# mLSTM heads: exponential from PSUM, row spread by one float32r product, last head in two parts, diagonal masked by a minimum on VectorE

## The reference, cut to what matters

```python
lf = jax.nn.log_sigmoid(f_pre)                       # bb: its running sum
log_d = bb[..., :, None] - bb[..., None, :] + ib[..., None, :]
log_d = jnp.where(tri, log_d, -jnp.inf)
m_t = jnp.maximum(log_inter, jnp.max(log_d, axis=-1))
w_intra = jnp.exp(log_d - m_t[..., None])
s = jnp.einsum('bhtd,bhsd->bhts', qb, kb) * w_intra
num = ... + jnp.einsum('bhts,bhse->bhte', s, vb)
den = ... + jnp.sum(s, axis=-1)
h = num / jnp.maximum(jnp.abs(den), jnp.exp(-m_t))[..., None]
hh = rmsnorm(hh.transpose(0, 2, 1, 3), head_g)
return (hh * jax.nn.sigmoid(og)) @ w_out
```

## Time and profile before

| | us |
|---|---|
| median of 3 runs | 2892.79 (2875.12 to 2896.78) |
| profiled execution | 2877.44 |
| its span | 2875.7 |
| TensorE busy | 2755.7 (96%) |
| VectorE busy | 1515.8 (53%) |
| ScalarE busy | 866.6 (30%) |
| GpSimd busy | 357.9 (12%) |
| the heads' stage, from its first instruction to the next stage | 87.7 |

### The profile page before, as it was taken

One profiled execution on the slowest core, in us unless ns is written; L12 is line 12 of the kernel. 1 busy time (PEld: TensorE's weight loads), 2 busy tenths in 40 slices (PEclk: granted clock), 3 DMA queues, 4 the chain that ended last, 5 costly groups with the idle time before them and its releaser, 6 DMA issues. The chain is left out here.

```text
span 2875.7 us, 38965 instructions
## 1 busy us (share of the span) xinstructions
PE 2755.7 (96%) x16683; PEld 2189.1 (76%) x16683; DVE 1515.8 (53%) x2117; ACT 866.6 (30%) x1156; POOL 357.9 (12%) x334
## 2 busy tenths in 40 slices
PE   7999999899899999999999998999999899999998
PEld 5888878588675787788887875788887665788887
DVE  4555454689757634555545325452454655452433
ACT  3222233422343222322123435322222434422221
POOL 1111010211100000111100002120121100120110
PEclk9999999899999999999999997999999999999999
DMA  5554542000211123455553210233342200233231
GB/s 154 156 175 153 170 138 62 25 4 4 83 45 44 37 88 96 131 164 169 161 164 119 88 60 3 71 103 110 110 148 94 81 31 1 73 103 103 88 103 59
DMA packets 264316, 271.14 MB, mean 94 GB/s; under 512 B 9631, under 2 KB 245126, under 8 KB 263951
## 3 DMA queue, kind: packets, MB, share of 16 engines
q1 hardware_dynamic: 248784, 206.78, 23.6%
q0 software_dynamic: 15360, 61.87, 6.4%
HBM read 266.53 MB, written 2.10 MB: 93 GB/s over the span
## 5 line engine op out<-in xcount | busy, mean ns | idle before, releaser
L920 DVE TENSOR_TENSOR mix_wl<-ring_raw,mix_wh 128x2048 fp32r<-128x2048 f32 (+2 forms) x66 | 153.1, 2319 | 221.6 <-ACT mix_wh L807 221.5
L707 PE MATMUL mix_ps<-h_mix_hi,mix_wh 128*128 128x512 f32 x624 | 244.9, 392 | 0.0
L709 PE MATMUL mix_ps<-h_mix_lo,mix_wh 128*128 128x512 f32 x624 | 243.0, 389 | 0.0
L807 ACT ACTIVATE mix_wh<-ring_raw 128x2048 fp32r<-128x2048 f32 (+2 forms) x66 | 117.6, 1782 | 212.5 <-PE mix_ps L713 162.1
L707 PE MATMUL ffn_ps<-h_rw_hi,ffn_wh 128*128 128x512 f32 x448 | 175.4, 392 | 0.0
L709 PE MATMUL ffn_ps<-h_rw_lo,ffn_wh 128*128 128x512 f32 x448 | 174.3, 389 | 0.0
L920 DVE TENSOR_TENSOR mlp_wl<-ring_raw,mlp_wh 128x2048 fp32r<-128x2048 f32 (+1 forms) x38 | 96.7, 2545 | 130.3 <-ACT mlp_wh L807 130.3
L920 DVE TENSOR_TENSOR mlp_wl<-mlp_raw,mlp_wh 128x2048 fp32r<-128x2048 f32 x36 | 93.2, 2589 | 133.2 <-ACT mlp_wh L807 133.2
L713 PE MATMUL mix_ps<-h_mix_hi,mix_wl 128*128 128x512 f32 x624 | 154.2, 389 | 0.0
L707 PE MATMUL mlp_ps<-view,mlp_wh 128*128 128x512 f32 x384 | 149.8, 390 | 0.0
L709 PE MATMUL mlp_ps<-view,mlp_wh 128*128 128x512 f32 x384 | 149.5, 389 | 0.0
(11 more groups left out here) (605 smaller groups left out, 6107.5 us busy)
## 6 DMA issues: line engine op xcount, KB each, us to landing
ring_raw<-in_mlp_w SPq DMA_DIRECT2D x32, 1024.0 KB, 5.3
mlp_raw<-in_mlp_w SPq DMA_DIRECT2D x32, 1024.0 KB, 5.2
ffn_sraw<-in_ada_w POOLq DMA_DIRECT2D x34, 768.0 KB, 5.2
ffn_raw<-in_ffn_w_gu SPq DMA_DIRECT2D x44, 512.0 KB, 5.2
ring_raw<-in_ffn_w_gu SPq DMA_DIRECT2D x44, 512.0 KB, 4.8
mix_sraw<-in_ada_w POOLq DMA_DIRECT2D x22, 768.0 KB, 5.2
ring_raw<-in_w_in SPq DMA_DIRECT2D x14, 1024.0 KB, 5.3
ring_raw<-in_a_w_in SPq DMA_DIRECT2D x12, 1024.0 KB, 5.3
```

The lines of the kernel that those rows point to most:

```text
L707: nc.tensor.matmul(ps[:, it.banks[t], :], w(h, k, t), xh[:, k, :], start=it.first and k == it.k0, stop=False)
L709: nc.tensor.matmul(ps[:, it.banks[t], :], w(h, k, t), xl[:, k, :], start=False, stop=False)
L807: nc.scalar.activation(slot(wh, it), slot(raw, it), ACT.Copy).then_inc(hi_ready, 1)
L920: nc.vector.tensor_tensor(slot(wl, it), slot(raw, it), slot(wh, it).bitcast(F32), ALU.subtract)\
```

## The change

- The row -M is split in the gates' stage into a high part (float32r) in partitions 0 to 7 and the remainder in partitions 32 to 39, over a cleared tile. One float32r product with a selector of 40 rows (`sel2`) spreads both and adds them. The selector, the triangle and the floors as columns (`fcol`) are prepared in the gates' stage instead of at the start of the heads.
- ScalarE takes the exponential directly from the spread row in PSUM, with the column c[s] as its bias. The argument on VectorE and the copy `negM` are gone; `dT` has six buffers.
- The diagonal block of `dT`, not of `pT`, is cut by a minimum with the 0/1 triangle, on VectorE, two units ahead. GpSimd has nothing to do in the stage. The largest valid exponential is 1.
- Columns, and the reciprocal, are computed once per group, in groups of heads 0-2, 3-4, 5-6 and 7. Seven tables give the places of broadcasts, turns, copies, squares, roots, columns, scales and gates.
- The last head is done in two halves; its second half is read from PSUM. The sqrt table is loaded by an activation on one column after the last exponential. 3 keep-clock products stand at the start instead of 4 and 6, and 4 before the last turns.

```diff
@@ mlstm_gates
+            if at == first + 5:
+                sp.wait_ge(act_done, 6)
+                sp.dma_start(sel_in, I["c_sel2"]).then_inc(sel_loaded, 16)
+                sp.dma_start(causal, I["c_causal"]).then_inc(sel_loaded, 16)
...
+            if at == first + 5:
+                eng.wait_ge(floors, 2)
+                for t in range(TT):
+                    last = nc.tensor.transpose(pf[:, t, :], floor_rows[:, t * P:(t + 1) * P], e.ident[0:H, 0:H])
+                last.then_inc(turned, 1)
...
+            if at == first + 5:
+                eng.wait_ge(turned, 2)
+                nc.scalar.activation(fcol[:, :, :].rearrange("p h t -> p t h"), pf[:, :, :], ACT.Copy)
+            if at == first + 8:
+                eng.wait_ge(sel_loaded, 32)
+                nc.scalar.activation(sel, sel_in, ACT.Copy)
...
-                nc.vector.tensor_scalar(rows[:, 0, :], M[:, :], -1.0, None, ALU.mult).then_inc(dve_done, 1)
+                then(eng, nc.vector.memset(parts.bitcast(F32), 0.0))
+                nc.vector.tensor_scalar(neg[:, :], M[:, :], -1.0, None, ALU.mult).then_inc(dve_done, 1)
+            if at == first + 4:
+                eng.wait_ge(dve_done, 2)
+                then(eng, nc.vector.tensor_copy(parts[0:H, :], neg[:, :]))
+                nc.vector.tensor_tensor(parts[32:32 + H, :], neg[:, :], parts[0:H, :].bitcast(F32), ALU.subtract)
@@ tables
-MH_GROUPS = ((0, 1, 2), (3, 4), (5, 6, 7))
-MH_ROOTS = {(4, 0): 0, (6, 0): 1}
-MH_TURNS = {(4, 2): 0, (5, 0): 1, (5, 2): 2, (6, 2): 3, (7, 0): 4}
+MH_GROUPS = ((0, 1, 2), (3, 4), (5, 6), (7,))
+MH_BROADCASTS = {(0, 0): (1,), (0, 3): (2,), (2, 0): (3,), (3, 1): (4,), (4, 2): (5,), (5, 2): (6,), (6, 0): (7,)}
+MH_TURNS = {(4, 3): (0,), (5, 2): (1,), (6, 3): (2,), (7, 0): (3, 4), (7, 2): (5,)}
+MH_TAKES = {(2, 1): 0, (3, 0): 1, (3, 2): 2, (4, 3): 3, (5, 1): 4, (6, 3): 5, (7, 1): 6}
+MH_SQUARES = {(2, 2): 0, (3, 2): 1, (3, 3): 2, (5, 1): 3, (5, 3): 4, (7, 0): 5, (7, 2): 6}
+MH_ROOTS = {(4, 3): 0, (6, 3): 1}
+MH_COLUMNS = {(3, 2): 0, (5, 3): 1, (7, 1): 2}
+MH_SCALES = {(4, 2): (0,), (5, 1): (1, 2), (6, 2): (3, 4), (7, 2): (5, 6)}
+MH_GATES = {(5, 0): 0, (6, 2): 1, (6, 3): 2, (7, 0): 3, (7, 1): 4}
@@ mlstm_heads, tensor
                 if h > 0:
-                    pe.wait_ge(rows_out, h)
-                nc.tensor.matmul(pm[:, :], sel[:, h, :], rows[:, 0, :], start=True, stop=True).then_inc(rows_done, 1)
+                    pe.wait_ge(d_ready, TT * h)
+                nc.tensor.matmul(pm[:, :], sel[:, h * P:(h + 1) * P], parts, start=True, stop=True).then_inc(rows_done, 1)
...
-            for t in range(TT):
-                last = nc.tensor.transpose(pt[:, t * H:(t + 1) * H], rows[:, 1, t * P:(t + 1) * P], e.ident[0:H, 0:H])
-            last.then_inc(floors, 1)
-            keep_clock(nc, e, pn[:, 1, 1, :], 4)
-            pe.wait_ge(loaded, 32)
             broadcast(0)
             scores(0)
             scores(1)
-            keep_clock(nc, e, pn[:, 1, 1, :], 6)
+            keep_clock(nc, e, pn[:, 1, 1, :], 3)
...
-                pe.wait_ge(p_masked, n + 1)
+                pe.wait_ge(p_ready, n + 1)
...
-            for k in left:
-                turn(k)
+            pe.wait_ge(scaled, end)
+            turn(end - 1)
+            keep_clock(nc, e, pS[:, 1, :], 4)
+            for half in range(2):
+                pe.wait_ge(scaled, end + half + 1)
+                turn(end, (2 * half, 2 * half + 1))
@@ mlstm_heads, scalar
+                act.wait_ge(rows_done, h + 1)
+                if n >= ARGS:
+                    act.wait_ge(p_ready, n - ARGS + 1)
+                nc.scalar.activation(dT[:, n % ARGS, j * P:L], pm[:, j * P:L], ACT.Exp, bias=ccol[:, j, h:h + 1])\
+                    .then_inc(d_ready, 1)
+                if n + 1 == len(units):
+                    nc.scalar.activation(warm[:, :], e.eps[:, 0:1], ACT.Sqrt)
...
+            root(2)
+            act.wait_ge(used, TT * end + 2)
+            nc.scalar.activation(outT[:, end, 0:2, :], blocks_of(end)[:, 0, :, :], ACT.Copy).then_inc(taken, 1)
+            for i in range(2):
+                square(end, i, blocks_of(end)[:, 0, i, 0:P])
+            act.wait_ge(last_taken, 1)
+            for i in range(2):
+                square(end, 2 + i, blocks_of(end)[:, 1, i, 0:P])
+            root(3)
@@ mlstm_heads, vector
-                nc.vector.tensor_scalar(dT[:, n % 3, j * P:L], negM[:, h % 2, j * P:L], ccol[:, j, h:h + 1], 0.0,
-                                        ALU.add, ALU.min).then_inc(arg_ready, 1)
+            def mask(n):
+                dve.wait_ge(d_ready, n + 1)
+                j = units[n][1]
+                diag = dT[:, n % ARGS, j * P:(j + 1) * P]
+                nc.vector.tensor_tensor(diag, diag, causal, ALU.min).then_inc(d_masked, 1)
...
+            gate(end - 2)
+            dve.wait_ge(used, TT * H)
+            nc.vector.tensor_copy(outT[:, end, 2:4, P], blocks_of(end)[:, 1, :, P]).then_inc(last_taken, 1)
+            dve.wait_ge(last_taken, 1)
+            columns(3)
+            gate(end - 1)
+            scale(end, slice(0, 2))
+            scale(end, slice(2, TT), blocks_of(end)[:, 1, :, 0:P])
+            gate(end)
@@ mlstm_heads, gpsimd: the block is gone
-                nc.gpsimd.tensor_tensor(diag, diag, causal[:, :], ALU.mult).then_inc(p_masked, 1)
```

More of the change, by code:

```diff
@@ L1229, in shape_tables @@
     t["c_sel"] = sel.reshape(A_HEADS, -1)
+    sel2 = np.zeros((ROW_PARTS, A_HEADS * P), f32)
+    for part in range(2):
+        sel2[32 * part:32 * part + A_HEADS] = t["c_sel"]
+    t["c_sel2"] = sel2
     inv = (10000.0 ** (-np.arange(32, dtype=f32).astype(np.float64) / 32)).astype(f32)
@@ L2692, in mlstm_heads @@
     group_of = {h: g for g, hs in enumerate(MH_GROUPS) for h in hs}
-    left = [h for h in range(H) if h not in MH_TURNS.values()]
+    end = H - 1
     with ExitStack() as s:
         sb, pb, sem = opened(nc, s, "mh", 34)
-        sel, causal = sb("sel", [H, H, P]), sb("causal", [P, P])
-        dT, pT = sb("dT", [P, 3, L]), sb("pT", [P, 3, L])
-        negM, sq = sb("negM", [P, 2, L]), sb("sq", [P, P])
+        dT, pT, sq = sb("dT", [P, ARGS, L]), sb("pT", [P, 3, L]), sb("sq", [P, 2, P])
         outT = sb("outT", [P, H, TT, W])
-        fcol, mag = sb("fcol", [P, TT, H]), sb("mag", [P, 2, TT])
+        mag, warm = sb("mag", [P, 3, TT]), sb("warm", [P, 1])
@@ L2753, in _ @@
             scores(1)
-            keep_clock(nc, e, pn[:, 1, 1, :], 6)
+            keep_clock(nc, e, pn[:, 1, 1, :], 3)
             pe.wait_ge(ones_ready, 1)
-            pe.wait_ge(floors_out, 1)
             for n, (h, j) in enumerate(units):
-                if j == 0 and h + 1 < H:
-                    broadcast(h + 1)
+                for k in MH_BROADCASTS.get((h, j), ()):
+                    broadcast(k)
+                for k in MH_TURNS.get((h, j), ()):
+                    pe.wait_ge(scaled, k + 1)
+                    turn(k)
                 if n + 2 < len(units):
                     scores(n + 2)
-                if n > 0 and units[n - 1] in MH_TURNS:
-                    turn(MH_TURNS[units[n - 1]])
-                pe.wait_ge(p_masked, n + 1)
+                pe.wait_ge(p_ready, n + 1)
                 if j == 0 and h >= 2:
@@ L2820, in _ @@
-            root(len(MH_GROUPS) - 1)
+                if (h, j) in MH_SQUARES:
+                    k = MH_SQUARES[h, j]
+                    act.wait_ge(taken, k + 1)
+                    for i in range(TT):
+                        square(k, i, outT[:, k, i, 0:P])
+                if (h, j) in MH_TAKES:
+                    take(MH_TAKES[h, j])
+            root(2)
+            act.wait_ge(used, TT * end + 2)
+            nc.scalar.activation(outT[:, end, 0:2, :], blocks_of(end)[:, 0, :, :], ACT.Copy).then_inc(taken, 1)
@@ L2834, in columns @@
                 then(nc.vector.scalar_tensor_tensor(m, m, EPS, m, ALU.mult, ALU.mult))
-                dve.wait_ge(squared, TT * (h + 1))
-                then(nc.vector.scalar_tensor_tensor(c, mean[:, h, :], 1.0 / P, m, ALU.mult, ALU.add))
-                g = group_of[h]
-                hs = MH_GROUPS[g]
-                if h == hs[-1]:
-                    part = rs[:, hs[0]:h + 1, :]
-                    nc.vector.reciprocal(part, part).then_inc(inv_ready, 1)
-            def scale(k):
+                dve.wait_ge(squared, TT * hs.stop)
@@ L2844, in scale @@
+                then(nc.vector.scalar_tensor_tensor(c, mean[:, hs, :], 1.0 / P, m, ALU.mult, ALU.add))
+                nc.vector.reciprocal(c, c).then_inc(inv_ready, 1)
+            def scale(k, tiles=slice(0, TT), src=None):
                 dve.wait_ge(rs_ready, group_of[k] + 1)
-                d = outT[:, k, :, 0:P]
-                nc.vector.tensor_tensor(d, d, rs[:, k, :].unsqueeze(2).to_broadcast([P, TT, P]), ALU.mult)\
+                d, n = outT[:, k, tiles, 0:P], tiles.stop - tiles.start
```

(1 more changed line is left out.)

140 lines of the change are left out of this document (52 added, 88 removed).

## The result

| | before | changed |
|---|---|---|
| median of 4 runs | 2888.13 (2875.12 to 2896.78) | 2847.86 (2845.96 to 2848.33) |
| profiled execution | 2877.44 | 2848.33 |
| its span, mean granted clock | 2875.7, 0.978 | 2846.5, 0.986 |
| the heads' stage in it | 87.7 | 63.4 |

The stage itself came out close to the forecast: 24.3 us shorter, where the sum for it was 25.0, or 23.4 with what was given back to the clock. Here are its stretches in the changed kernel, in the form of the earlier trace rows: the start up to the second broadcast, the unit loop up to the last product, the tail, and the first 10 us of the next stage.

A forecast was written before the change was run, and what follows sets the result against it. TensorE's stream was taken to pace full-clock heads, other engines' chain the tail. Gains 4.4 + 10.1 + 4.2 + 0.4 + 5.9 - 0.4 = 24.6, less 1.6 for clock, gave 23 us: median 2870, range 2850 to 2884.

The forecast's parts named there:

- given back to the clock: Heads' stage: 1.6 us taken off the gain because head 7's new 1.7 us stand might lower the clock.
- the base: Whole kernel: gains reckoned on the profiled 2877.4 us, its 15.4 us difference carried to the median of 2892.8 us.
- the gain is larger than the trace can show: Rival, chance 0.27: slow runs' extra 16 to 20 us partly this stage's clock, or a low new median; 2854 to 2863.
- Faster by over 1%: Whole-kernel outcome, chance 0.29, against 0.69 for within 1% and 0.02 for slower by over 1%.
- Start: Start of the heads' stage: 8.29 us falls to 3.9, gain 4.4, with constants and floors ready beforehand.
- the stand: Head 7: TensorE stands 1.7 us before head 4's turn, which needs the gate of head 3.
- tail: End of the heads' stage: 10.91 us falls to 5.05, gain 5.9, with the sqrt table already in.
- 7.8 us of clock in heads 1 and 2: Heads 0 to 2: 7.8 of the 10.1 us gain is clock, if the clock stays up.
- leaves the chain: Heads: GpSimd's 0.46 us per diagonal block leaves the chain from VectorE to TensorE; VectorE's minimum taken as 0.28 us.
- either fits a head of 6.25 us: ScalarE in the heads: exponential from PSUM, bounded by 0.52 and somewhat over 0.6 us, fits; TensorE sets the pace.
- 0.4 paid in the gates' stage: Stage before the heads: four more 8-row transposes on TensorE cost 0.4 us; clear, DMAs and copy cost nothing.
- The rule on the clock: TensorE: idle time throttles, activity releases; a start without a stand then keeps the full 23 us, otherwise 16.

The follow-up runs named there:

- the 101: All executions of the unedited kernel before with a clock on record, from 2860.3 to 2904.1 us, median 2877.0 us.
- e_start: Changed kernel with the old start: constants awaited by DMA, 4 and 6 keep-clock products; 2856.1 us, ratio to before 0.9921.
- e_f32both: Changed kernel with the diagonal cut on GpSimd, head 4's turn one unit later and a float32 broadcast; 2847.8 us, ratio to before 0.9889.
- b_keep: Kernel before with 9 keep-clock products in its tail and one behind each of its three turns; 2874.3 us, ratio to before 1.0006.
- e_pool: Changed kernel with the diagonal block cut on GpSimd again, as a product with the 0/1 triangle; 2846.8 us, ratio to before 0.9913.
- e_copy: Changed kernel with the exponential taken from an SBUF copy of the row, one ScalarE copy per head; 2864.8 us, ratio to before 0.9955.
- v_turn: Changed kernel with the turn of head 4 one unit later, at (7,1); 2844.9 us, ratio to before 0.9890.
- b_again: Kernel before, run again without edit; 2879.9 us, ratio to before 1.0024.
- a_again: Changed kernel, run again without edit; 2851.8 us, ratio to before 0.9911.
- a_third: Changed kernel, run a third time without edit; 2850.8 us, ratio to before 0.9896.
- e_f32bc: Changed kernel with the row spread by a float32 product instead of float32r; 2866.6 us, ratio to before 0.9971.
- e_nokeep: Changed kernel without the 4 keep-clock products ahead of the last turns; 2850.1 us, ratio to before 0.9898.

## Why the prediction was wrong

**The step that failed is the base.** "It lies 15.4 us under the median of the runs, 2892.8 us; I carry the difference to the median." The profiled execution, 2877.4, was a typical one of the 101, whose median is 2877.0. Two of the three runs took 2893 and 2897 us; their clocks are not on record, but the executions of the 101 that take as long have clocks of 0.967 to 0.973, so a low clock in these two is the likely reason. Without the carrying the same sum of gains is the 2854 that the prediction gives for a profiled execution; the median of 17 runs is 2849.3. Moreover the traces of the changed kernel have less low clock (82 to 89 us of the span, against 127 and 130), so a surplus that is clock has no reason to be added to it. The rival "the gain is larger than the trace can show" named the doubt and got 0.27, but its own figures, 2854 to 2863, missed too. Its reason is half shown: the surplus goes with the clock, but the low stretches lie all over the program and not only in this stage. "Faster by over 1%" had 0.29; the first four runs say so with 1.4%, all 17 with 0.96% do not.

**The steps of the stage held in the main.** Start 3.9 forecast, 3.4 measured (the two scores take 1.6 and not 1.85); broadcast 0.3, measured 0.31 to 0.43; minimum 0.28, measured 0.285; heads 0 to 6 45.9 in sum, measured 45.5; the stand 1.7, measured 1.70; tail 5.05, measured 4.25. A head was taken as 6.25, and those in the dense part took 5.95 to 6.32, but one, between the 512-column scores of heads 5 and 6, took 8.93. The sum of the stage was 25.0, 23.4 with what was given back to the clock; measured 24.3. In head 7 the clock took 3.0, nearly twice the 1.6 allowed, the start and the tail gave 1.3 more, and the heads at full clock 1.1 more.

**Four readings inside it were too simple.** The 7.8 us of clock in heads 1 and 2 were counted as a gain of the change. No single part that was tested brings or removes the stretch: without the new start (e_start) or with the float32 broadcast (e_f32both) it stays away, with the new broadcast in the old heads it only moves, and b_keep lost most of it without any edit there. That the shorter stream makes it rarer fits the runs' clocks but is not shown. Second, moving the diagonal from GpSimd, which "leaves the chain", to VectorE was counted as costing nothing; e_pool puts it at 2.2 us. Third, ScalarE's "either fits a head of 6.25 us" rested on its mean load; e_copy shows that the order of its queue decides. Fourth, the stand of 1.7 us came as worked out, but it is not what makes head 7 long: v_turn takes it away and gains 0.3 us.

**The term that was missing** is the clock outside the stage. Of 29.1 us of span, 24.3 lie in the stage, 2.3 in the stage behind it (0.9 shown above, the rest likely), 4.0 in low stretches after that, and 1.6 were lost before the stage. The 2.3 come again between b_again and a_again and between before and a_third. The 4.0 do not (0.5 and 1.6 there), so they are the luck of this pair of traces. The 1.6 lost before the stage are mostly drift too: the new kernel is 1.5 us late already in the first dense products, at 49 us, and the heads begin anywhere from 1699.1 to 1705.8 us in the sixteen traces.

The 0.4 paid in the gates' stage is 0.6, the same in all three pairs: the products on either side of the floors' four transposes move apart by 0.59 us. In the changed kernel:

```profile
1638.00 0.41 PE L2634 MATMUL mix_rs<-ident,view 8*128 8x8 f32 x4
1638.34 0.50 PE L670 MATMUL mix_ps<-mix_wh,h_mix_hi 128*128 128x512 f32 x1
```

The clear on VectorE takes 0.48 us and delays nothing: TensorE has no idle time before the first four transposes in either kernel, and the slack of 1.2 us that was read from the earlier trace rows shrinks to 0.55.

**Work and clock.** At a clock of 0.985, by the line of the runs above and with its slope for both, the two kernels stand at 2862.4 and 2849.5. That makes 12.9 us of work and 15 of clock, with a caution: filling idle time raises the mean clock without making the kernel much faster, as b_keep shows, which at that clock stands at 2866.1. Against b_keep the changed kernel is 16.6 us ahead at equal clock, in line with their stages (79.3 us, of which about 1.6 is clock, against 60.3). So the work is worth 13 to 17 us and the clock 11 to 15.

**The rule on the clock.** The Trainium skill (TensorE: Matmul & The Clock Gate, Part 1: The HAM clock gate) has idle time throttle and activity release. Of the falls seen here those in the changed kernel's head 7, in e_copy and in e_f32bc stand at or behind a stand of 1.70, 2.38 and 1.06 us, and so agree; the same 1.70 us in a_third and e_nokeep brought none, and before's heads 1 and 2 and the starts of the two kernels with the float32 broadcast fell with no idle time. The rule says where a fall is likelier, not that one comes.

## What to carry to other kernels

Before a difference between a profiled run and a median is carried anywhere, fit a line to the runs' time against their mean granted clock: if that takes the spread away, the base is the execution at the median clock of many runs, not the median of three. Cost a step moved onto a half-idle engine in the stage where its queue is fullest (here the heads with scale, gate and columns), and not by its share of busy time. And when a stand is taken away, look whether the end moves: in v_turn it did not.

By its traces the fastest version is e_pool, with or without the later turn: a stage of 58.1 us, 2.2 below the best trace of the changed kernel, and medians of 2846.8 and 2845.8. Against the changed kernel's 2849.3 that is 3 us, in line with the traces, but less than these runs can tell apart; v_turn, with a stage of 60.1, has the lowest median of all, 2844.9.

## What the runs showed of the hardware

- TensorE's clock falls at different places in executions of one program. The mean over a span was 0.967 to 0.985 in 101 executions, whose times span 44 us, and the line on the clock leaves 1.8 us of scatter.
- At full clock a float32 broadcast of 512 columns takes 0.93 to 1.05 us until the next product starts, float32r 0.31 to 0.43.
- An exponential with the column as bias takes 0.69, 0.57, 0.48 and 0.37 us from PSUM for 512 to 128 columns, and 0.72, 0.60, 0.50 and 0.39 from SBUF in e_copy: reading PSUM costs nothing here. In the kernel before, where VectorE had made the argument, it took 0.62, 0.52, 0.41 and 0.29 from SBUF: the bias itself is about 0.1 us.
